# Chunked attention on TensorE: the scores of two tiles, then the transposes and values of two tiles

## The reference

```python
    def one_chunk(args):
        j, q_j = args
        k_j = lax.dynamic_slice_in_dim(k_pad, j * CHUNK, BAND, axis=1)
        v_j = lax.dynamic_slice_in_dim(v_pad, j * CHUNK, BAND, axis=1)
        s = jnp.einsum('bqhd,bkhd->bhqk', q_j, k_j) * scale + bias
        valid = kb >= (LEFT_CHUNKS - j) * CHUNK
        s = jnp.where(valid, s, jnp.float32(-1e30))
        p = jax.nn.softmax(s, axis=-1)
        return jnp.einsum('bhqk,bkhd->bqhd', p, v_j)
```

## Time and profile before

| | |
|---|---|
| median of 3 runs | 2445.79 us (2445.44 to 2445.95) |
| the profiled execution | 2447.55 us, its span 2445.7 us |
| PE busy | 2399.3 us of the span, 98% |
| DVE, ACT, POOL busy | 65%, 48%, 50% |
| attention stage | about 1491 us to 1753 us of the span |
| in the stage, T rows / V rows / max rows | 480 / 960 / 128 |

### The profile page before, as it was taken

How to read it: one execution, slowest core, us unless ns; L and a number is a source line. 1 busy time by engine, 2 the same in 40 slices (tenths; PEclk the granted TensorE clock), 3 DMA queues, 4 the chain that set the end, 5 groups by cost and what they waited for, 6 DMA issues and landing times.

```text
span 2445.7 us, 36010 instructions
## 1 busy us (share of the span) xinstructions
PE 2399.3 (98%) x13552; PEld 2052.2 (84%) x13552; DVE 1588.6 (65%) x2151; ACT 1173.4 (48%) x2308; POOL 1219.0 (50%) x883
## 2 busy tenths in 40 slices
PE   7999999999999999999999989999999999999999
PEld 6888898875588898899888878999988888788887
DVE  6975657588543386653766765777434489788864
ACT  5322223344544353322545555888634434888861
POOL 2545545430044455545545535766554446866664
PEclk9999999999999999999999999999999999999999
DMA  7554544493034345543433348565244343300034
GB/s 277 156 193 148 184 162 156 145 321 141 27 112 150 104 156 174 184 143 104 120 104 86 104 132 218 144 158 143 63 136 155 107 160 122 104 1 1 3 128 156
DMA packets 295724, 329.21 MB, mean 135 GB/s; under 512 B 88264, under 2 KB 226304, under 8 KB 293760
## 3 DMA queue, kind: packets, MB, share of 16 engines
q1 hardware_dynamic: 294080, 326.81, 41.7%
q10 hardware_dynamic: 1472, 0.10, 0.0%
HBM read 247.53 MB, written 79.33 MB: 134 GB/s over the span
## 4 chain that ended last, share of the span: by engine, by line
PE 82%; DVE 8%; ACT 3%; issue 3%; POOL 2%; DMA 1%; SPq 1%; DVEq 0%; ACTq 0%
PE ps L1234 22%; PE ps L1235 22%; PE ps L1236 22%; PE ps L1571 3%; PE ps L1742 2%; PE ps L1723 2%; PE ps L1486 2%; PE ps L1505 2%; PE ps L1499 1%; PE ps L1557 1%; DVE s_raw L2421 1%; POOL w_lo L1120 1%; PE ps L1254 1%; PE ps L1469 1%; PE ps L1442 1%
## 5 line engine op out<-in xcount | busy, mean ns | idle before, releaser
L1120 POOL TENSOR_TENSOR w_lo<-raw,w_hi 128x512 fp32r<-128x512 f32 (+1 forms) x450 | 649.3, 1452 | 804.3 <-ACT w_hi L1848 768.5
L1848 ACT ACTIVATE w_hi<-raw 128x512 fp32r<-128x512 f32 (+1 forms) x454 | 281.1, 628 | 784.7 <-PE ps L1236 624.3
L1234 PE MATMUL ps<-w_hi,s_hi 128*128 128x256 f32 (+2 forms) x832 | 263.7, 317 | 9.5 <-POOL w_lo L1120 9.0
L1235 PE MATMUL ps<-w_lo,s_hi 128*128 128x256 f32 (+2 forms) x832 | 262.8, 316 | 0.0
L1236 PE MATMUL ps<-w_hi,s_lo 128*128 128x256 f32 (+2 forms) x832 | 262.7, 316 | 0.0
L1120 POOL TENSOR_TENSOR w_lo<-raw_wide,w_hi 128x512 fp32r<-128x512 f32 x112 | 157.2, 1413 | 149.5 <-ACT w_hi L1848 149.5
L2539 DVE TENSOR_TENSOR u<-u,ps 128x1024 f32<-128x1024 f32 (+1 forms) x96 | 116.4, 1212 | 148.2 <-PE ps L1236 144.7
L1234 PE MATMUL ps<-w_hi,a_hi 128*128 128x256 f32 (+2 forms) x624 | 197.0, 316 | 1.0 <-POOL w_lo L1120 1.0
L1235 PE MATMUL ps<-w_lo,a_hi 128*128 128x256 f32 (+2 forms) x624 | 196.6, 315 | 0.0
L1236 PE MATMUL ps<-w_hi,a_lo 128*128 128x256 f32 (+2 forms) x624 | 196.6, 315 | 0.0
L1234 PE MATMUL ps<-s_hi,w_hi 128*128 128x512 f32 x480 | 188.7, 393 | 3.2 <-DVE s_lo L2408 2.3
(11 more groups left out here) (346 smaller groups left out, 6242.1 us busy)
## 6 DMA issues: line engine op xcount, KB each, us to landing
raw<-in_w SPq DMA_DIRECT2D x158, 512.0 KB, 4.2
ada_c<-in_ada SPq DMA_DIRECT2D x14, 2304.0 KB, 11.0
blk<-u SPq DMA_DIRECT2D x46, 512.0 KB, 4.3
raw_wide<-in_w SPq DMA_DIRECT2D x32, 512.0 KB, 4.6
blk<-c SPq DMA_DIRECT2D x23, 512.0 KB, 3.3
blk<-m1s SPq DMA_DIRECT2D x23, 512.0 KB, 3.3
ada_first<-in_ada SPq DMA_DIRECT2D x12, 768.0 KB, 16.1
r_g<-blk SPq DMA_DIRECT2D x8, 1024.0 KB, 9.6
```

Source lines behind the costliest of these rows:

```text
L1120: pool.tensor_tensor(w_ring(w_lo, n), w_source(n), w_ring(w_hi, n).bitcast(F32), ALU.subtract)\
L1234: pe.matmul(out, a_hi_, b_hi_, start=first, stop=False, skip_group_check=True)
L1235: pe.matmul(out, a_hi_, b_lo_, start=False, stop=False, skip_group_check=True)
L1848: act.activation(w_ring(w_hi, n), w_source(n), ACT.Copy).then_inc(w_rounded, 1)
```

## The change

On PE, the scores are issued in pairs. From step 2 on, an even step e issues S(e + 3) and S(e + 4) ahead of T(e), and an odd step issues no scores. No instruction is added or removed, and the queues of the other engines stay as they are.

```diff
                 a_scores(2)
                 for e in range(AH * NT):
-                    if e + 3 < AH * NT:
+                    if e < 2:
                         a_scores(e + 3)
+                    elif e % 2 == 0:
+                        for ahead in range(e + 3, min(e + 5, AH * NT)):
+                            a_scores(ahead)
                     if e == 0:
                         pe.wait_ge(ev, evicted(27, "c12"))
                     a_turn(e)
```

## The result

The changed kernel takes 2452.25 us (median of 11 runs) against 2445.95 of the kernel before. The ratio is 1.002, with a 95% interval of 1.0012 to 1.0027, which is 2.9 to 6.6 us. The medians differ by 6.3 us, and the ratio stands for 4.9. The direction was as forecast; the size is about half of the 11.3 us of the sum.

A forecast was written before the change was run, and what follows sets the result against it. PE was taken to bound the kernel. Seven plain heads at 0.98 (6.9), five split heads at 0.72 (3.6) and 0.8 for heads 1 and 2 gave 11.3 us, so 2457.1; worked-out range 2453.5 to 2460.5, widened to 2449.5 to 2462.

The forecast's parts named there:

- PE's own work: nothing: PE's matmuls: the same ones run, grouping priced at nothing; at most 5.1 us back if kind changes cost 0.08 us.
- The wait at S(B + 6), 0.75 us: Early in each head, PE waits 0.70 us for DVE's 3.41 us chain from V(B - 1), 0.75 with slower restart.
- The wait at S(B + 9), 0.23 us: Later in each head, PE arrives sooner while DVE's low 3 keeps its place: PE waits 0.23 us.
- the lower bound's case: If low 3 takes low 1's 0.93 us, the S(B + 9) waits vanish: 12 x 0.23 = 2.8 us less.
- The paragraph on the shared pair: DVE low parts beside POOL: rows show 0.28 us lateness; the skill's blocking rule would make the sum 23.8; rows kept.
- S(B + 8), just in time: In plain heads, DVE's maximum is ready at 7.38 us from V(B - 1), PE arrives at 7.44: no wait.
- Split heads, net 0.72: Five heads with an output split: 0.75 + 0.41 + 0.23 of waits, less 0.67 no longer lost: 0.72 us each.
- Heads 1, 2, 14 and 15, 0.8: Stage's ends: 0.8 us for heads 1 and 2 together; head 14 counts as plain, head 15 adds nothing.
- the 1.29 us at T(19): Sign in head 2: PE's existing 1.29 us wait for POOL at T(19) would still be there.
- No change: Rival: DVE's chain is shorter or the lookahead covers it; 2446 within 2 us; chance 0.13.
- faster: Rival: fewer changes between values and scores pay 5.1 us and S(B + 6) does not wait; 2440.7; chance 0.05.
- much slower: Rival: waits of 0.7 us drop PE's clock, 12 us on top over 12 heads; 2469; chance 0.05.

The follow-up runs named there:

- gate_late: Changed kernel with DVE taking gate 1 behind max(B + 4) instead of ahead of low 1: 2450.58 us, ratio 1.0014 to the kernel before.
- p2_off: Changed kernel without the pairing at i = 2, so S(B + 6) stands behind T(B + 2) and V(B + 1) again: 2449.49 us, ratio 1.0011 to before.
- pool_beside: Changed kernel with POOL's bias operation one step later from head 3 and two added POOL multiplications ahead of prob(B + 2): 2460.73 us, ratio 1.0055 to before.
- bias_early: Changed kernel with POOL's bias operation one step earlier, placing prob(B + 2) beside low 1: 2452.6 us, ratio 1.0025 to before.
- both_loads: Changed kernel with gate 1 behind max(B + 4), the output split at i = 7 and the next head's queries and keys loaded earlier: 2442.95 us, ratio 0.9985 to before.
- both_late: Changed kernel with gate 1 behind max(B + 4) and the output split at i = 7 instead of 3: 2447.37 us, ratio 1.0003 to before.
- split_late: Changed kernel with DVE's output split at i = 7 instead of 3 in odd heads 5 to 13: 2449.86 us, ratio 1.0011 to before.

## Why the prediction was off, step by step

- **PE's own work: nothing.** Right. PE's 15.39 us a head without waits and 15.51 grouped, of which 0.10 is a located wait with its restart, leave next to nothing for the changes of kind; four fewer a head at 0.08 us would have shown as 0.3 us less.
- **The wait at S(B + 6), 0.75 us.** The place, the chain and who waits were right (gate_late and p2_off remove it; gate 1's idle time grew). The failed step is the sentence that DVE's chain from V(B - 1) is unchanged in its queue and takes 3.41 us. The queue was unchanged, the length of low 1 was not: 0.68 instead of 0.93, so that the chain takes 3.15 us. The wait measured 0.45 instead of 0.70, with the slower restart about 0.53 in a plain head (15.94 against 15.41).
- **The wait at S(B + 9), 0.23 us.** Wrong, the same error. Low 3 does not keep its length when it starts later beside the same operation of POOL; it ends 0.54 us behind that operation. It took 0.90 us, so the lower bound's case (low 3 at 0.93, no wait) is what came. V(67) to S(73) took 2.25 us, no wait. Seven plain heads at 0.98 should have been seven at 0.53: 3.2 us of the miss.
- **The paragraph on the shared pair.** This is where the error was made. The Trainium skill's rule ("SBUF — State Buffer", Who interferes with whom), that the engine that issues first has the shared pair for its whole instruction and the other is blocked, agrees with what pool_beside and bias_early show for POOL's multiplications: low 1 ends 0.55 us after the multiplication, at 1.27 and 0.80 us. It does not agree for POOL's bias operation: in the kernel before, low 1 ends at 1630.87, 0.55 us before that operation does, and there the measurement decides. I held it against the rows as a flat surcharge of 0.28 us and kept the lengths of the rows. The 0.93 was no bare length either: against the 0.68 us that low 1 takes alone, low 3 was late by 0.53. But the rows only fit together if low 3's end is tied to POOL's end, which prob(70)'s row would have told. The sum of 23.8 that I built on the rule had the wrong sign: moving two queues against each other took overlap away here.
- **S(B + 8), just in time.** Right in plain heads that PE does not wait (7.22 us behind V(63)), but not by so little: low 2 met no multiplication and took 0.75 us instead of 1.09, and max(70) ended 6.83 us behind V(63), not 7.33. In both_loads, where PE comes earlier, it is the last thing that PE meets.
- **Split heads, net 0.72.** Measured 16.45 against 16.13 us from V(55) to V(63), 0.32. The wait at S(B + 8) was there (0.40 to 0.43 against 0.36, and 0.50 against 0.41 with the restart), and so was the loss of 0.67 that falls away; the other two terms were too large as above: 5 x 0.4 = 2 us of the miss.
- **Heads 1, 2, 14 and 15, 0.8.** From the start to V(23) the changed kernel is 1.50 us later, 0.53 of it S(28), now ahead of V(23): 0.97. Near the 0.8, but this part moves by more than that between kernels, so it is not shown. One sign was missed: the 1.29 us at T(19) were to be still there, and it is 0.69.
- **Left out.** Head 12 lost 0.4 us to the load before (15.80 against 15.39) and takes 15.94 like its neighbours now. The new wait hides it: 0.4 of the miss.
- **Sum.** 3.2 + 2 + 0.4 = 5.6 us less than the 11.3 gives 5.7, against 5.9 in the span. The parts are read from the same two traces as the span, so this says where the miss lies and is no further test.
- **The rivals.** No change and faster are out. The granted clock of the changed kernel was 1.00 (2.4 GHz) from 1551 to 1745 us, with a wait of 0.45 us in each head, so much slower is out too.

## What to carry to other kernels

Reordering one engine's queue can change the length of instructions on other engines. Where two engines share something, carry over from a trace the time at which the other's operation ends, and not the duration of the one beside it. And issuing work earlier on the engine that sets the pace costs a wait wherever an item that it now asks for sooner has too little time to spare: list, for each moved piece, the item it waits for, and subtract what moved between on both sides. Here undoing the cause of old waits (the output split, the late load) gave 4 us without any grouping.

## What the runs showed of the hardware

A DVE subtraction with two operands of 128x512 in SBUF, started while POOL's multiplication ran, ended 0.54 to 0.55 us after that operation's end, at remaining times of 0.14 to 0.95 us (226 of 226); alone it took 0.68. The split of the outputs (two operands of 128x1024) ended 1.08 us after the multiplication, at remaining times of 0.38, 0.80 and 0.99 us, and took 1.46, 1.88 and 2.07; with no multiplication running when it started it took 1.20 to 1.21 (both_late). It goes the other way too: prob(60) started 0.34 us into the split and took 1.81 us, ending 0.68 us after it, and 0.83 in split_late, where the split stands elsewhere. POOL's bias operation (one operand from SBUF) did not hold a low part to its end: low 1 started 0.33 us into it and took 0.93, started 0.63 or 0.86 us into it and took 0.68, with more than 0.9 us of it still to run. What it holds and for how long was not tried.
